# A gated recurrence inside a trunk layer: VectorE's running sums first in their tick, ScalarE's mean squares last, one root for two heads, outputs in three PSUM banks instead of two

## What is computed

```
z = modulate(x) @ w_in                       # split into the inputs of two mixers and two gates
mixer A: gated linear attention, 4 heads, dk 128, dv 256
    h0 -> per token: h = exp(log_a) * h + k (x) v ;  o = q . h
    o = rmsnorm(o, gla_gain) * silu(gr)      # gr: a projection of the same input
mixer B: differential attention, 8 heads
x = x + gt1 * (sigmoid(g_a) * y_a + sigmoid(g_b) * y_b) @ w_out
x = x + gt2 * peer_ffn(modulate(x))          # per token 8 heads x 16 experts of 16384 rows
```

## Time and profile before

| | us |
|---|---|
| median of 3 runs | 4300.85 |
| lowest, highest | 4298.69, 4303.13 |
| span of the profiled execution | 4303.9 |
| busy: TensorE / VectorE / ScalarE / POOL | 3099.8 / 2705.5 / 1511.1 / 1254.2 |

### The profile page before, as it was taken

How to read it: one execution, slowest core, us unless ns; L and a number is a source line. 1 busy time by engine, 2 the same in 40 slices (tenths; PEclk the granted TensorE clock), 3 DMA queues, 4 the chain that set the end, 5 groups by cost and what they waited for, 6 DMA issues and landing times. The chain is left out here.

```text
span 4303.9 us, 48708 instructions
## 1 busy us (share of the span) xinstructions
PE 3099.8 (72%) x15864; PEld 1982.7 (46%) x15864; DVE 2705.5 (63%) x7617; ACT 1511.1 (35%) x3085; POOL 1254.2 (29%) x1068
## 2 busy tenths in 40 slices
PE   6787798887788769778887679768776677733333
PEld 4676565665555337455554347444433254400000
DVE  1326357337667884477668873577678945776775
ACT  3533366312255651114555540223446611010010
POOL 0000111112233332333223332333334323355553
PEclk8888888898888779898888889888778788855555
DMA  7485767687989989998999899989999999999998
GB/s 261 157 305 189 278 243 267 254 319 307 357 343 375 360 309 390 404 415 354 363 362 366 351 359 384 417 344 402 375 372 386 363 410 415 398 408 415 416 406 336
DMA packets 269363, 1499.17 MB, mean 348 GB/s; under 512 B 44968, under 2 KB 81672, under 8 KB 97464
## 3 DMA queue, kind: packets, MB, share of 16 engines
q0 software_dynamic: 152064, 1107.36, 64.5%
q1 hardware_dynamic: 117048, 388.70, 24.0%
HBM read 1463.49 MB, written 31.36 MB: 347 GB/s over the span
## 5 line engine op out<-in xcount | busy, mean ns | idle before, releaser
L1698 POOL DMA_INDIRECT rt_ring<-in_peer_uv,rt_few_idx x1056 | 1250.9, 1185 | 3021.0 <-PE rt_acc L876 2385.5
L1644 DVE SCALAR_TENSOR_TENSOR rt_ring<-rt_ring,rt_h 128x1024 f32<-128x1024 f32 x1056 | 1265.9, 1220 | 504.7 <-DMA rt_ring<-in_peer_uv,rt_few_idx 481.7
L876 PE MATMUL rt_acc<-rt_ring,rt_diag 128*32 128x512 f32 x4224 | 759.9, 795 | 623.1 <-DVE rt_diag L1655 622.1
L625 PE MATMUL pair<-dense,w 128*128 128x256 f32 (+2 forms) x3056 | 598.6, 355 | 14.0 <-DMA w<-in_weights 12.2
L625 PEld LDWEIGHTS pair<-dense,w 128*128 128x128 f32 x3056 | 518.1, 199 | 128.8 <-issue 64.5
L614 PE MATMUL pair<-w,dense 128*128 128x256 f32 (+1 forms) x2352 | 556.4, 395 | 9.5 <-DVE dense L1300 3.5
L1199 ACT ACTIVATE rt_act_dot<-rt_dot 128x2 f32<-128x2 f32 x528 | 106.1, 202 | 1269.0 <-DVE rt_ring L1644 1262.1
L876 PEld LDWEIGHTS rt_acc<-rt_ring,rt_diag 128*32 128x32 f32 x4224 | 100.1, 122 | 953.4 <-DVE rt_diag L1655 810.1
L614 PEld LDWEIGHTS pair<-w,dense 128*128 128x128 f32 (+1 forms) x2352 | 436.2, 189 | 158.8 <-issue 72.9
L1655 DVE TENSOR_SCALAR rt_diag<-cst,rt_act_dot,rt_few_prob 128x32 f32<-128x32 f32 x1056 | 266.1, 296 | 119.9 <-ACT rt_act_dot L1199 109.5
L625 PE MATMUL bank<-dense,w 128*128 128x256 f32 (+2 forms) x1424 | 276.9, 351 | 1.7 <-DMA w<-in_weights 1.2
(11 more groups left out here) (241 smaller groups left out, 3248.5 us busy)
## 6 DMA issues: line engine op xcount, KB each, us to landing
w<-in_weights SPq DMA_DIRECT2D x284, 1024.0 KB
rt_ring<-in_peer_uv,rt_few_idx POOLq DMA_INDIRECT x1056
dense<-scratch_mod SPq DMA_DIRECT2D x18, 512.0 KB, 12.4
dense<-in_x_prompt SPq DMA_DIRECT2D x16, 512.0 KB, 13.5
rt_h<-scratch_h SPq DMA_DIRECT2D x33, 128.0 KB
rt_x<-scratch_x SPq DMA_DIRECT2D x132, 32.0 KB
out_k_prompt<-dense SPq DMA_DIRECT2D x32, 128.0 KB
out_v_prompt<-dense SPq DMA_DIRECT2D x32, 128.0 KB
```

What stands on the lines that cost most here:

```text
L625: mm = nc.tensor.matmul(bank[b][:, 0:n], wt[:, k * CH + j * P:k * CH + (j + 1) * P], src[:, k, 0:n], start=(k == 0), stop=(k == KC - 1))
L876: mm = nc.tensor.matmul(acc[u % 2][a * T:(a + 1) * T, :], diag[b % 2][:, i, :], slot[:, D + c * BANK:D + (c + 1) * BANK], start=(q == 0), ...
L1644: dt = nc.vector.scalar_tensor_tensor(up, up, 1.0, h2[u % 2][:], ALU.mult, ALU.mult, accum_out=dot[:, b % 2, i:i + 1])
L1698: nc.gpsimd.indirect_dma_start(ring[n % RING][:], None, d["peer_uv"], bass.IndirectOffsetOnAxis(ap=few_idx[u % 2][:, c:c + 1], axis=0)).th ...
```

## The change

Four things change. VectorE's running sums (scan and block sums) come first in a tick. ScalarE's mean square comes last, and Ln and Exp run only after the second unit of a pair (both heads of a tile), on two columns at once. VectorE's gains of a pair run together in the tick after that (odd ticks from 5 on). The outputs go to banks 2, 5 and 4 in turn.

```diff
 TensorE, gla
-  bo, before = take(("go", g, p, t, j), [(2, 5)[(base + x) % 2]])
+  bo, before = take(("go", g, p, t, j), [(2, 5, 4)[(base + x) % 3]])
 ScalarE, gla
...
-                if 0 <= k - 3 < len(units):
-                    x = k - 3
-                    ti, t, c0, n, j = units[x]
-                    c = x % 2
-                    b, before = sessions["go", g, p, t, j]
-                    act.wait_ge(bank_made[b], before + 1)
-                    act.wait_ge(gl_squared, base + x)
-                    nc.scalar.activation(gsq[0:n, :], bank[b][0:n, 0:GDV], ACT.Square, scale=GDV ** -0.5,
-                                         accum_out=gms[0:n, c:c + 1]).then_inc(gl_squared, 1)
-                    act.wait_ge(gl_squared, base + x + 1)
-                    settle(nc.scalar.activation(gln[0:n, c:c + 1], gms[0:n, c:c + 1], ACT.Ln, bias=eps[0:n, :]))
-                    nc.scalar.activation(grstd[0:n, c:c + 1], gln[0:n, c:c + 1], ACT.Exp, scale=-0.5).then_inc(gl_rstd, 1)
                 if k < len(units):
...
                     ex.then_inc(gl_decays, 1)
+                if 0 <= k - 3 < len(units):
+                    x = k - 3
...
+                    nc.scalar.activation(gsq[0:n, :], bank[b][0:n, 0:GDV], ACT.Square, scale=GDV ** -0.5,
+                                         accum_out=gms[0:n, c:c + 1]).then_inc(gl_squared, 1)
+                    if c == 1:
+                        act.wait_ge(gl_squared, base + x + 1)
+                        settle(nc.scalar.activation(gln[0:n, :], gms[0:n, :], ACT.Ln, bias=eps[0:n, :]))
+                        nc.scalar.activation(grstd[0:n, :], gln[0:n, :], ACT.Exp, scale=-0.5).then_inc(gl_rstd, 2)
 VectorE, gla
...
-                if 0 <= k - 4 < len(units):
-                    x = k - 4
+                if k < len(units):
+                    ti, t, c0, n, j = units[k]
+                    c = k % 2
+                    if k >= 2:
+                        dve.wait_ge(gl_decays, base + k - 1)
+                    settle(nc.vector.tensor_tensor_scan(cum[:, c, 1:n + 1], one[:].to_broadcast([P, n]), glT[:, j, c0:c0 + n],
+                                                        0.0, ALU.mult, ALU.add))
...
+                for x in range(k - 5, k - 3) if k % 2 == 1 and 0 <= k - 5 < len(units) else ():
                     ti, t, c0, n, j = units[x]
                     b, before = sessions["go", g, p, t, j]
                     dve.wait_ge(gl_rstd, base + x + 1)
...
```

More of the change, by code:

```diff
@@ L1101, in gla @@
                     ex.then_inc(gl_decays, 1)
+                if 0 <= k - 3 < len(units):
+                    x = k - 3
+                    ti, t, c0, n, j = units[x]
+                    c = x % 2
+                    b, before = sessions["go", g, p, t, j]
+                    act.wait_ge(bank_made[b], before + 1)
+                    act.wait_ge(gl_squared, base + x)
+                    nc.scalar.activation(gsq[0:n, :], bank[b][0:n, 0:GDV], ACT.Square, scale=GDV ** -0.5,
[4 more added lines that the diff above has]
+                        nc.scalar.activation(grstd[0:n, :], gln[0:n, :], ACT.Exp, scale=-0.5).then_inc(gl_rstd, 2)
             def gla_gate(g, p, i):
@@ L1386, in gla @@
                         settle(nc.vector.memset(cum, 0.0))
-                if 0 <= k - 4 < len(units):
-                    x = k - 4
+                if k < len(units):
[5 more added lines that the diff above has]
+                                                        0.0, ALU.mult, ALU.add))
+                    start = cum[:, c, 0:n].rearrange("p (b c) -> p b c", c=GBLK)[:, :, 0:1].to_broadcast([P, n // GBLK, GBLK])
+                    nc.vector.tensor_tensor(blk[:, c, 0:n].rearrange("p (b c) -> p b c", c=GBLK),
+                                            cum[:, c, 1:n + 1].rearrange("p (b c) -> p b c", c=GBLK), start,
+                                            ALU.subtract).then_inc(gl_blocked, 1)
+                for x in range(k - 5, k - 3) if k % 2 == 1 and 0 <= k - 5 < len(units) else ():
                     ti, t, c0, n, j = units[x]
@@ L1421, in gla @@
                     nc.vector.tensor_tensor(e_end[:, c, 0:n], kk, e_end[:, c, 0:n], ALU.mult).then_inc(gl_keyed, 1)
-                if k < len(units):
-                    ti, t, c0, n, j = units[k]
-                    c = k % 2
-                    if k >= 2:
-                        dve.wait_ge(gl_decays, base + k - 1)
-                    settle(nc.vector.tensor_tensor_scan(cum[:, c, 1:n + 1], one[:].to_broadcast([P, n]), glT[:, j, c0:c0 + n],
-                                                        0.0, ALU.mult, ALU.add))
-                    start = cum[:, c, 0:n].rearrange("p (b c) -> p b c", c=GBLK)[:, :, 0:1].to_broadcast([P, n // GBLK, GBLK])
-                    nc.vector.tensor_tensor(blk[:, c, 0:n].rearrange("p (b c) -> p b c", c=GBLK),
-                                            cum[:, c, 1:n + 1].rearrange("p (b c) -> p b c", c=GBLK), start,
-                                            ALU.subtract).then_inc(gl_blocked, 1)
             def gla_gate(g, p, i):
```

## The result

| | before | changed |
|---|---|---|
| median, us | 4301.99 (4 runs) | 4277.37 (4 runs) |
| lowest, highest | 4298.69, 4305.71 | 4265.25, 4282.50 |
| span of the profiled execution | 4303.9 | 4280.7 |
| ratio of times, 95% interval | | 0.9933, 0.9915 to 0.9952 |

Faster by 24.6 us between the medians, by 0.67% (21 to 37 us) with the interval. The forecast was 4286, 15 us faster, the range 4268 to 4305. The sign and the range hold; the size is short by 10 us (between the medians) to 14 us (by the ratio).

A forecast was written before the change was run, and what follows sets the result against it. No engine is full: tile 0's path bounds until 437 us, then engines in recurrence passes and transfers where only gathers remain. -13.2 - 6.0 + 1.1 = -18.1 us, times 0.8 about -15, gives 4286 us, range 4268 to 4305.

The forecast's parts named there:

- ScalarE's saving: Recurrence passes: 37 table loads (47.5 us) and 18 Ln/Exp pairs (8.8 us) go, 56.3 us, the gain's upper bound.
- Six four-head passes: Groups 1 to 3: 2.2 us less a pass, 13.2 us in all, ends 0 and 3.9 a pass.
- the pass worked through: Second pass of group 2: 1.3 to 2.6 us shorter, the fourth output complete 1.3 us earlier.
- tick 1: Four-head pass: sums ahead of the first head's products delay these up to 0.7 us; ScalarE gets its exponentials' input earlier.
- Tick 3: Four-head pass: no root ahead of the exponentials, 3.10 us saved and 1.28 added for a load.
- Group 4: Four passes of tiles 7 and 8: 1.5 us less each, 6 us in all, ends 0 and 3.1 a pass.
- Tile 0: First pass gains 2.5 us at its first gate projection, second loses 3.6 waiting for the paired gain: 1.1 us slower.
- The factor 0.8: Whole sum: transfers behind a pass take some back, so 0.8 of 18.1 us counts, about 15 us.
- The third bank at nothing: Output banks: the third costed at nothing, as each output's bank was freed in the tick before it was needed.
- The gathers did not take it back: Rival, passes: ScalarE's saved time becomes waiting for transfers, only 1 to 5 us faster, 4296 to 4300; chance 0.27.
- The gates met the paired gains: Rival, pass ends: gate projections wait for a bank the paired gain frees, 3.6 us each, 4313 to 4320; chance 0.12.
- All of it shows: Rival: TensorE's last wait, 3.9 us, goes in six passes and 3.1 in four, 4266; chance 0.08.

The follow-up runs named there:

- e10: The changed kernel with ScalarE's mean square and paired root back ahead of the exponentials: 4281.61 us, ratio 0.9956 to the kernel before.
- e3: The kernel before with paired root, paired gains and three banks, both orders within a tick old: 4289.99 us, ratio 0.9966.
- e9: The changed kernel with VectorE's running sums back at the end of their tick: 4295.28 us, ratio 0.9990 to the kernel before.
- e1: The kernel before with VectorE's running sums first in their tick, nothing else: 4297.79 us, ratio 0.9991.
- e7: The kernel before with running sums first and mean square last, but a root for each head and two banks: 4309.14 us, ratio 1.0013.
- e4: The changed kernel with the outputs in banks 2 and 5 in turn, as before: 4308.3 us, ratio 1.0017 to the kernel before.
- c1: The kernel before, unchanged, timed and profiled once more: 4301.96 us, ratio 1.0001.
- c2: The changed kernel as it is, measured once more on another chip: 4269.29 us, ratio 0.9924 to the kernel before.
- e8: The kernel before with a third output bank and nothing else: 4305.57 us, ratio 1.0002.
- e5: The changed kernel with group 0 alone on two output banks: 4278.6 us, ratio 0.9938 to the kernel before.
- e6: The changed kernel with Ln and Exp of the recurrence's root replaced by two copies: 4271.37 us, ratio 0.9931 to the kernel before.
- e11: The changed kernel with group 0 alone on two banks, measured again on another chip: 4273.27 us, ratio 0.9935 to the kernel before.

## Why the prediction was right, and where it was too small

**ScalarE's saving**: right. 37 loads by 1.283 us as counted, 54.1 us of busy time against 56.3. I called it the gain's upper bound. It bounds what the removed instructions can give, but not what VectorE's new order gives: e10 takes no instruction from ScalarE beyond e3 and its passes are 14 us shorter.

**Six four-head passes, 2.2 us each, 13.2 us**: this is the step that failed, in its size. The mean of the three old sums is 208.1 us, of the two profiles of the change 184.5: 23.6 us, 3.9 us a pass. That is the upper end that I had kept (3.9), though not by the way I gave it, so the match is luck: I took TensorE's last wait as the whole of what could go. In the pass worked through the end went as forecast: from the fourth output to the diagonals behind it I had 1.3 us less (2.6 less 1.3), and measured 1.2. It was the fourth output that I had only 1.3 us earlier, and it was complete 4.9 us earlier.

The error is in the sentences on tick 1. There I set down the sums' new place as 0.7 us lost for the products of the first head, with something in return for ScalarE that I gave no number. It is the 2.7 us by which the third set of exponentials starts earlier (in e9, with the sums last, it starts after 8.13 us, as before). Tick 3 came out right in size: of the fourth set's 4.4 us it adds 1.8, which is 3.10 less 1.28; but I took the exponentials to start as soon as the root was gone, and e9 shows that they do so only with the sums first. The waits for running sums that stood in the trace of before, 37.6 us over the span and 5.0 us in this very pass, I had not read. They say that ScalarE's exponentials were held by VectorE's order in ticks 1 and 2 and by the root from tick 3 on. e9 and e3 show the price: with the pairing but the sums last the six passes give 9.5 us (208.1 less the mean of 198.8 and 198.4), 1.6 a pass, and the running sums first add 14.1 (alone, in e1, 3.6).

**TensorE's clock**: a term that was missing. I added up the lengths of the recurrence's own TensorE instructions (L705, L706, L711, L719, L724) in the rows of the six passes: 152.3, 146.1 and 146.2 us in the three profiles with the old passes, 136.1 and 132.1 in those of the change, for the same instructions. Scores that took 3.43 us take 1.93, as in the rows of the pass above. These are 14 us less, TensorE at the higher clock more of the time. How much of the 23.6 us they are isn't shown, since an instruction that ends sooner can be followed by a longer wait: e7 has 141.8 us in passes as long as before (208.9), and e4 142.9 us in the longest passes of all. What lets the clock be higher I can't show either.

**Group 4, 1.5 us each, 6 us**: not shown. The waits for diagonals of the earlier trace rows are 2.29 and 3.81 after the change, 2.71 and 3.55 before. The two stretches sum to 96.4, 89.3 and 93.3 in the profiles of the old passes and to 90.2 and 91.6 in the change, 2 us less, within the scatter.

**Tile 0**: both halves right. First pass, TensorE's timeline beside the earlier trace rows:

```profile
122.94 0.59 PE L711 MATMUL pair<-dense 128*128 128x256 f32 x2
124.20 3.69 PE L614 MATMUL pair<-w,dense 128*128 128x256 f32 x16 [0.67 <-DVE state L1411]
```

The projection starts 2.3 us earlier after the first scores (11.58 instead of 13.87), 2.5 were forecast, and takes 3.69 instead of 5.38, 1.7 us more, because the clock had not fallen: before, the window from 124 to 126 us, behind the idle 3.06 us, has a granted clock of 0.50, and in the change it is 1.00 from 121 to 131 us. The second pass loses 3.5 us to the gain, 3.6 were forecast, and 3.7 with all (16.9 instead of 13.2). POOL's wait of 437.2 us is 440.3 in one profile and 434.5 in the other: no loss and no gain that can be told (c1 has 436.9).

**The factor 0.8**: wrong, if slightly. -23.6 - 2 and tile 0 at -0.3 make -26, and the times show 24.6 (first medians) to 34 (c2 beside its own before). In the end nothing is missing. VectorE's waits for transfers grew:

```profile
DVE rt_ring L1644 <- DMA rt_ring<-in_peer_uv,rt_few_idx: 493.7, 347, 6.6
```

(481.7 before, and 459.0 in c1 against 507.1 in c2), and the gather steps behind the passes kept most of their lead: against the first profile of before, c2 is 25 us ahead at the end of group 2 (22 us against c1) and 29 at the start of group 4 (23 against c1). Only behind group 3 does a part come back: from the step at 2300 us to that at 2883 us the lead falls from 35 to 29 us in c2 and from 16 to 14 in the first profile of the change. Since e8 and e9, which led by little or nothing, are 4 and 8 us slower than before in that stretch, this too is within the scatter of profiles.

**The third bank at nothing**: right alone (e8) and wrong in this change. I read the rows of before, where no output waits for a gain, and didn't ask how long the paired gain would hold a bank. With two banks the same change is slower than before (e4). It would have made no difference to the sum, as the bank is part of the change; but it is what kept the change from being slower.

**The rivals.** The gathers did not take it back; ScalarE's low share of 35% said nothing about the passes. The Trainium skill (Perfetto Trace Analysis, section Identifying the Most-Contended Engine) says to optimize the most-contended engine first. I had read from it that an edit that relieves ScalarE gives nothing here; this case disagrees with that reading, with ratios of 0.9966 (e3) and 0.9933. The gates met the paired gains once, in tile 0, and not in groups 2 to 4, where the weighted sums ahead of them in TensorE's queue (from 1351.07 to 1352.1 in the pass above) are not done before the gains are (1351.8). "All of it shows", 4266 with a chance of 0.08, was close to c2's 4269 by its number, but not by its way: it had TensorE's last waits for the source, and 12.4 us from group 4, which isn't shown.

## What to carry to other kernels

When an instruction is taken away from an in-order queue, ask what its successor waits for otherwise: the root's place was taken by a wait for running sums that the root had hidden, and once the pairing was in, moving those sums gave more than the pairing had (14 us to 9.5 in the passes; moved alone, 3.6). List every wait of the stage in the trace of before, not only the ones that the removed work is named in. Work that is batched holds its buffers longer, so count the buffers for the batch and not for what waits today: without one more PSUM bank this gain of 0.7% was a loss of 0.2%. And take two profiles before reading a stretch for less than 10 us.

## What the runs showed of the hardware that I had not expected

TensorE's clock came back at different moments after the same work of TensorE. Windows of the second pass of group 1, the first half of it, before and after the change (from the left: window, length, busy of TensorE, its weight loads, VectorE, ScalarE, POOL, granted clock, DMA share, GB/s):

```profile
617.50:621.50 4.00, 3.91 (x12) 2.76 (x12) 3.15 (x15) 3.95 (x8) 0.00 (x0) 0.50 0.00 0
621.50:625.50 4.00, 4.00 (x22) 3.45 (x24) 3.42 (x12) 3.33 (x15) 0.00 (x0) 0.50 0.00 0
```

```profile
617.60:621.60 4.00, 3.91 (x12) 2.76 (x12) 3.17 (x13) 3.95 (x8) 0.00 (x0) 0.50 0.12 51
621.60:625.60 4.00, 4.00 (x31) 2.94 (x30) 3.92 (x17) 3.99 (x20) 0.60 (x1) 0.95 0.00 0
```

TensorE had idled 5.6 us in both ahead of the pass and then done the same instructions, 3.9 us busy of 4 in the first window, at the lower of its two levels, 1.2 GHz. Then the granted clock is 0.95 of 2.4 GHz in the one and stays at 0.50 in the other. The second scores of this pass take 1.9 to 2.2 us in all profiles of the change, of e3, e5, e6, e10 and e11, and 3.4 us in all of before, c1, e1, e4, e7, e8 and e9. In this pass it repeats in both profiles of either kernel, so it doesn't look like chance; what in the kernels decides it isn't settled. In other passes it doesn't repeat: the third scores of the second pass of group 2 take 2.36 us in the first profile of before and 3.44 in c1.
